# Attention in a hybrid decoder step: the masked chunk first, a running row maximum, value products spread over two rows, two tile banks swapped

## The chip, the cores and the metric

The kernel runs on one core of a Trainium2 chip. The core has TensorE (PE, matmuls; its weight loads are listed as PEld), VectorE (DVE), ScalarE (ACT), GpSimd (POOL) and SyncE (SP), which run side by side and wait for each other through semaphores. Results of matmuls land in eight PSUM banks of 512 fp32 columns. The metric is the time of one execution on the device in microseconds; lower is better.

## The reference, cut to what matters

The program is one inference step with two layers. Each layer runs over a prompt of 2048 tokens (and eight single tokens with their caches). One input projection feeds four head groups: a short convolution, RWKV-7 time mixing, latent attention, and attention into 256 memory tokens; then an output projection and the residual. The part that is changed is the causal latent attention of the prompt, four heads:

```
s = q_lat . ckv + q_rope . krope                     # for every head, query block, key
s = where(kpos <= qpos, s * MLA_SCALE, -1e30)
pr = softmax(s, axis=keys)
o = pr . ckv                                         # then through w_uv, times a SiLU gate
```

The kernel folds w_uk and w_uv into keys and values (`keysT`, 96 rows for each head; `vals`, 64 columns for each head), and it divides by the sum of the exponentials after the products. All data is fp32.

## The kernel before

**Blocks.** A layer goes over the prompt in 8 blocks of 256 tokens. Block number = 2m + e, with m = 0 to 3 and e = 0 or 1, so there are 16 prompt blocks in the program, four for each m. A block is projected (27 tiles of the input projection, `tile`), then comes RWKV in chunks, with the later tiles and the query work put between its steps (`rest`), then the attention, the memory attention and the output projection. Each engine has its own program in the order of its own text; the order is written by hand and is kept by semaphores.

**Attention of a block.** It has 8 rows: `row = 4p + 2j + h`, with p the head pair, j the half of the 256 tokens (128 queries) and h the head of the pair. h = 0 is the even-head row, h = 1 the odd-head row that follows it. A row has m + 1 chunks of up to 512 keys; chunks are counted through, c = 0 to 8(m+1) - 1, and `chunk_of` gives c's row and its key chunk kc. The last key chunk, kc = m, holds the causal diagonal: its width is (2e + j + 1) * 128, and the last 128 columns get a mask (`fmask`). So for e = 0 that chunk is 128 or 256 wide, for e = 1 384 or 512.

For chunk c the work is:
- TensorE, `scores(c)`: one matmul of up to 512 columns (two instructions) into one of five banks. Five are issued ahead; `scores(c + 5)` follows `turn(c)`.
- VectorE, `masked_max(c)`: if it is the masked chunk, add the mask in the bank (L1640); reduce to the maximum of the chunk (L1642); after the row's last chunk reduce over the chunks (L1645) and scale by -MLA_SCALE (L1647), which signals `s_an`, with a drain between these.
- ScalarE, `probs(c)` (L2251): exponential with the row's maximum as bias, into `Sm`. It waits for `s_an` of its row, and so for the scores of all chunks of it.
- TensorE, `turn(c)` (L660): up to four 128x128 transposes of `Sm`.
- ScalarE, `take(c)`: copy of the turned chunk out of PSUM, for an even row to `PTe` (room for whole rows), for an odd row to `PT`, two buffers (L2261). ScalarE's order is probs(0), then for each c probs(c + 1), take(c).
- TensorE, `values(c)`: for a chunk of an odd row the value products of both heads of the pair, up to eight matmuls in two column halves, accumulated in bank 4. On TensorE the order is, for each c: turn(c), scores(c + 5), values(c - 1), so products stand in the odd-head rows alone.

**Banks of the tiles.** Tiles 15 to 24 alternate between banks 6 and 7, `6 + (t - 15) % 2`, so tile 19 is in bank 6, tile 20 in bank 7. In `rest`, just ahead of tile 19 (its eight matmuls begin at s = 34), the latents are turned into bank 7 (s = 28 to 31, read by ScalarE at L2215 and L2216, first `s_krt`) and the value rows are made in bank 6 (s = 32, 33, read at L2222, second `s_krt`). Tile 19 waits for the second, tile 20 for the first. ScalarE does, in this order: L2215, L2216, two DMA issues (L2219), `level(2)` (two copies at L2185, which TensorE's `second_product` of that level waits for), L2222.

On the chip all matmuls stand at L656 (transposes at L660), since a helper records them; the tiles' names tell them apart: `bank<-kv,Q` are scores, `bank<-PT,kv`, `bank<-T,kv`, `bank<-pr,kv` value products, `bank<-cst,Sm` the transposes of probabilities, `bank<-hT,win` the input projection, `bank<-wuv,ckr` the value rows.

Of the kernel before, what the change touches and what calls it, by code (L numbers as in the profile page):

```python
# [15 lines left out]
ACT = mybir.ActivationFunctionType  # L16
AX = mybir.AxisListType.X
MULT, ADD, SUB, POW, MAX, MIN = ALU.mult, ALU.add, ALU.subtract, ALU.pow, ALU.max, ALU.min

P = 128  # L20
# [18 lines left out]
MLA_SCALE = (NOPE + RD) ** -0.5  # L39
# [108 lines left out]
def build_program(nc, a):  # L148
    ctx = ExitStack()
    with ctx:  # L150
# [5 lines left out]
        def sig(name, n, base=0):  # L156

            s = Sig(ctx, nc, name, n, base)
            if base:
# [41 lines left out]
        XX = sb("XX", [P, NH, 2, P])  # L201
# [16 lines left out]
        PP = [ctx.enter_context(nc.psum_tensor(f"bank{i}", [P, 512], F32)) for i in range(8)]  # L218
# [8 lines left out]
        flat4 = lambda t: t[:, :, :, :].rearrange("p a b t -> p (a b t)")  # L227
# [16 lines left out]
        OT = XX[:, :, :, :].rearrange("p h a t -> p h (a t)")  # L244
        ckvN = qd[:, 0, :].rearrange("p (t r) -> p t r", r=R)
        tmax, rmax, rneg = ml[:, 0:32].rearrange("p (r k) -> p r k", k=4), ml[:, 32:40], ml[:, 40:48]
        psum, rsum, rinv = ml[:, 48:80].rearrange("p (r k) -> p r k", k=4), ml[:, 80:88], ml[:, 88:96]
        inv64 = T3[:, :, :].rearrange("p a (b d) -> p (a b) d", d=64)
        whole = lambda t: t[:, :, :].rearrange("p a (b q) -> p a b q", b=2)
        PTe = [[whole(t) for t in (T1, T2, T3, eP)],  # L250
               [pr[:, 2 * i:2 * i + 2, 1:1 + T].rearrange("p a (b q) -> p a b q", b=2) for i in range(3)] + [whole(Ls)]]
# [97 lines left out]
        s_krt = sig("turned_latents_read", 2)  # L349
# [5 lines left out]
        s_an = sig("row_max_ready", 8)  # L355
# [30 lines left out]
        s_av = sig("values_summed", STEPS // 2, base=1)  # L386
# [61 lines left out]

        def chunk_of(c, m):

            row, kc = c // (m + 1), c % (m + 1)
            return row, kc, row // 4, row // 2 % 2, row % 2

        def chunk_width(B, c, m):

# [2 lines left out]

        def copies_of(c, m):

            row, kc, _, _, _ = chunk_of(c, m)
            return row // 2 * (m + 1) + kc

        def score_bank(c):

# [1 line left out]

        def tile_bank(t):

            return t % 4 if t < 15 else 6 + (t - 15) % 2 if t < 25 else 3  # L470

        def steps_before(l, m, e):

# [180 lines left out]
        def _(pe):  # L654
# [28 lines left out]
            def tile(B, t, k0=0, k1=KD):  # L683

                g, i, c, f = TILES[t]
                bank = tile_bank(t)
                if k0 == 0:
                    if i == 0:
                        pe.wait_ge(s_wi[g % 2].h, s_wi[g % 2].at(B.ip, loads_of_slot(g)))
                    if f == 64:  # L690
                        pe.wait_ge(s_kc.h, s_kc.at(B.ip, 1))
                    if 4 <= t < 15:
                        pe.wait_ge(s_pa.h, s_pa.at(B.ip, t - 3))
                    elif t == 15:
                        pe.wait_ge(s_rw.h, s_rw.at(B.it, 1))
                    elif t == 19:
                        pe.wait_ge(s_krt.h, s_krt.at(B.ip, 2))
                    elif t == 20:
                        pe.wait_ge(s_krt.h, s_krt.at(B.ip, 1))
                    elif t == 25:  # L700
                        pe.wait_ge(s_ar[1].h, pairs_done(B))
                    elif t == 26:
                        pe.wait_ge(s_pa.h, s_pa.at(B.ip, t))
                    elif t > 16:
                        pe.wait_ge(s_pa.h, s_pa.at(B.ip, t - 1))
                for k in range(k0, k1):
                    last = mm(PP[bank][0:f, 0:T + B.ns], win[:, g % 2, k, c:c + f], hT[:, k, 0:T + B.ns], k == 0, k == KD - 1)
                if k1 == KD:
                    last.then_inc(s_pj.h, 1)
# [255 lines left out]
            def attention(B, l, m, e):  # L965

                n0, n = steps_before(l, m, e), 8 * (m + 1)

                def scores(c):
                    _, kc, p, j, h = chunk_of(c, m)  # L970
                    w = chunk_width(B, c, m)
                    mm(PP[score_bank(c)][:, 0:w], Q96[:, 2 * p + h, j * P:(j + 1) * P],
                       keysT[:, 2 * p + h, kc * KC:kc * KC + w]).then_inc(s_as.h, 1)

                def turn(c):
                    pe.wait_ge(s_ae.h, n0 + c + 1)
                    if c >= 2:
                        pe.wait_ge(s_ar[chunk_of(c - 2, m)[4]].h, n0 // 2 + copies_of(c - 2, m) + 1)
                    for i in range(chunk_width(B, c, m) // P):
                        last = tr(PP[2 + c % 2][:, i * P:(i + 1) * P], Sm[:, c % 2, i * P:(i + 1) * P], P)  # L980
                    last.then_inc(s_at.h, 1)

                def values(c):
                    _, kc, p, j, h = chunk_of(c, m)
                    if h == 0:
                        return
                    x = copies_of(c, m)
                    pe.wait_ge(s_ar[0].h, n0 // 2 + x + 1)
                    pe.wait_ge(s_ar[1].h, n0 // 2 + x + 1)
                    even, odd = PTe[(2 * p + j) % 2][kc], PT[:, x % 2, :, :]  # L990
                    k = chunk_width(B, c, m) // P
                    o = slice((2 * p + j) * P, (2 * p + j + 1) * P)
                    for i in range(k):
                        first, final = kc == 0 and i == 0, kc == m and i == k - 1
                        v = vals[:, kc * 4 + i, 2 * p * HD:(2 * p + 2) * HD]
                        mm(PP[4][0:HD, o], v[:, 0:HD], even[:, i // 2, i % 2, :], first, final)
                        last = mm(PP[4][HD:P, o], v[:, HD:P], odd[:, i, :], first, final)
                    last.then_inc(s_av.h, 1)
                pe.wait_ge(s_kvd.h, s_kvd.at(B.it, 1))
                pe.wait_ge(s_krt.h, s_krt.at(B.ip, 2))  # L1000
                pe.wait_ge(s_pa.h, s_pa.at(B.ip, NTILES - 2))
                pe.wait_ge(s_yr.h, s_yr.at(B.ip, 4))
                for c in range(5):
                    scores(c)
                for c in range(n):
                    turn(c)
                    if c + 5 < n:
                        scores(c + 5)
                    if c:
                        values(c - 1)  # L1010
                values(n - 1)

            def attention_out(B):

# [269 lines left out]
        def _(v):  # L1284
            def drain():

                v.drain()  # L1287
# [343 lines left out]
            def attention(B, l, m, e):  # L1631

                n0, n = steps_before(l, m, e), 8 * (m + 1)

                def masked_max(c):
                    row, kc, _, _, _ = chunk_of(c, m)
                    w, bank = chunk_width(B, c, m), PP[score_bank(c)]
                    v.wait_ge(s_as.h, n0 + c + 1)
                    if kc == m:
                        v.tensor_tensor(bank[:, w - P:w], bank[:, w - P:w], fmask[:, :], ADD)  # L1640
                        drain()
                    v.tensor_reduce(tmax[:, row, kc:kc + 1], bank[:, 0:w], AX, MAX)  # L1642
                    if kc == m:
                        drain()
                        v.tensor_reduce(rmax[:, row:row + 1], tmax[:, row, 0:m + 1], AX, MAX)  # L1645
                        drain()
                        v.tensor_scalar(rneg[:, row:row + 1], rmax[:, row:row + 1], -MLA_SCALE, None, MULT).then_inc(s_an.h, 1)  # L1647

                for c in range(5):
                    masked_max(c)  # L1650
                for c in range(5, n):
                    masked_max(c)
                v.wait_ge(s_ae.h, n0 + n)
                v.tensor_reduce(rsum, psum[:, :, 0:m + 1], AX, ADD)
                drain()
                v.reciprocal(rinv, rsum)
                v.wait_ge(s_av.h, n0 // 2 + 3 * (m + 1) + s_av.base)
                drain()
                v.tensor_copy(inv64, scalars(rinv, 64)).then_inc(s_on.h, 1)
# [293 lines left out]
        def _(act):  # L1953
# [10 lines left out]
            for l in range(L):  # L1964
# [194 lines left out]
                def block(B, m, e):  # L2159
# [94 lines left out]
                    def take(c):  # L2254
# [1 line left out]
                        x, k = copies_of(c, m), chunk_width(B, c, m) // P  # L2256
                        act.wait_ge(s_at.h, n0 + c + 1 + s_at.base)
                        if h:
                            if x >= 2:
                                act.wait_ge(s_av.h, n0 // 2 + x - 1 + s_av.base)  # L2260
                            act.activation(PT[:, x % 2, 0:k, :], PP[2 + c % 2][:, 0:k * P].rearrange("p (a t) -> p a t", a=k), ACT.Copy)\  # L2261
                                .then_inc(s_ar[1].h, 1)
                            return
                        if 2 * p + j >= 2:
                            act.wait_ge(s_av.h, n0 // 2 + x - 2 * (m + 1) + 1 + s_av.base)
                        o, q = PTe[(2 * p + j) % 2][kc], PP[2 + c % 2][:, 0:k * P].rearrange("p (a t) -> p a t", t=P)
                        if k == 1:
                            last = act.activation(o[:, 0, 0, :], PP[2 + c % 2][:, 0:P], ACT.Copy)
                        elif k == 3:
# [192 lines left out]
```

## Time and profile before

| | |
|---|---|
| time, median of 3 runs | 4077.79 us (4076.91 to 4081.21) |
| profiled execution, its own time | 4085.56 us |
| its span in the profile | 4083.4 us |
| mean granted TensorE clock in it | 0.968 of full speed |
| busy: TensorE, weight loads, VectorE, ScalarE, GpSimd | 3745.4, 2727.1, 1823.1, 1373.2, 145.4 us |
| exponentials of the attention (L2251) | 320 |
| masks (L1640), reductions over a row's chunks (L1645), scalings (L1647) | 128 each |

Each engine's busy time is the sum of its instructions' records. A group of instructions shows after the bar its busy time, the mean of one in ns, and the idle time of the engine just before such instructions, with what ended it. A long idle time matters only where it stands on the engine that sets the pace.

### The profile page before, as it was taken

The page shows a single profiled execution, that of the slowest core. Times are in us where ns is not written, and L with a number is a line of the kernel's source. Part 1 is how long each engine was busy: PE and PEld are TensorE (multiplying, and loading weights), DVE is VectorE, ACT ScalarE, POOL GpSimd, SP SyncE. Part 2 cuts the span into 40 slices and gives each one's busy share as a digit, 9 for nine tenths or more (in the row PEclk, how much of TensorE's full clock was granted, in tenths as well). Part 3 has the DMA queues.
Part 4 walks back from the last instruction along what each step waited for, and adds up shares of the span by engine and source line. Part 5 has one row for each costly group of instructions (what it writes and reads, how often), then busy time and mean ns, then how long its engine had stood idle before and what let it go on. Part 6 is the DMA issues. An engine that isn't in the chain of part 4 may idle for free.

```text
span 4083.4 us, 73861 instructions
## 1 busy us (share of the span) xinstructions
PE 3745.4 (92%) x30760; PEld 2727.1 (67%) x30760; DVE 1823.1 (45%) x3987; ACT 1373.2 (34%) x3579; POOL 145.4 (4%) x278
## 2 busy tenths in 40 slices
PE   4978999999999999999789799999999999999996
PEld 3756767676767667586457477776767686766763
DVE  2544535454544435354325445353535454353542
ACT  1232333334242432434223224233333435234241
POOL 0000000000000000000000000000000000000000
PEclk8988999999999999999889799999999999999998
DMA  6323242423324142231433142524242331523203
GB/s 228 102 88 112 85 157 85 137 86 125 98 93 139 53 158 85 69 121 39 141 125 96 57 143 67 166 65 157 85 137 85 100 122 52 169 65 112 89 27 110
DMA packets 319400, 431.78 MB, mean 106 GB/s; under 512 B 26670, under 2 KB 276460, under 8 KB 318908
## 3 DMA queue, kind: packets, MB, share of 16 engines
q1 hardware_dynamic: 291672, 374.85, 28.7%
q0 software_dynamic: 11648, 41.95, 3.2%
q10 hardware_dynamic: 15748, 10.24, 0.9%
q8 instruction: 245, 4.01, 0.4%
q14 instruction: 87, 0.71, 0.1%
HBM read 405.22 MB, written 32.26 MB: 107 GB/s over the span
## 4 chain that ended last, share of the span: by engine, by line
PE 77%; DVE 8%; DMA 5%; ACT 4%; issue 3%; DVEq 3%; ACTq 1%; POOL 0%; SPq 0%; POOLq 0%
PE bank L656 70%; PE bank L660 7%; DMA wout<-in_w_out 4%; DVEq L1287 3%; DVE T L1391 1%; DVE ml L1642 1%; ACT Sm L2251 1%; DMA win<-in_w_in 0%; ACT PT L2291 0%; ACTq L2219 0%; ACT mix L2148 0%; DVE xin L1710 0%; ACT PT L2103 0%; DVE pr L1399 0%; DVE T L1401 0%
## 5 line engine op out<-in xcount | busy, mean ns | idle before, releaser
L656 PE MATMUL bank<-hT,win 128*128 128x256 f32 (+3 forms) x6912 | 1637.1, 387 | 20.6 <-ACT kv L2222 14.3
L656 PEld LDWEIGHTS bank<-hT,win 128*128 128x128 f32 (+1 forms) x6912 | 1266.8, 189 | 258.7 <-issue 60.9
L656 PE MATMUL bank<-wout,mix 128*128 128x512 f32 x1024 | 459.0, 598 | 35.6 <-DMA wout<-in_w_out 33.2
L656 PEld LDWEIGHTS bank<-wout,mix 128*128 128x128 f32 x1024 | 187.4, 190 | 285.5 <-issue 200.6
L1642 DVE TENSOR_REDUCE ml<-bank 128x1 f32<-128x512 f32 (+3 forms) x320 | 194.9, 610 | 211.6 <-PE bank L656 202.1
L656 PE MATMUL bank<-kv,Q 96*128 96x512 f32 (+3 forms) x640 | 276.8, 531 | 11.2 <-ACT mix L2017 11.2
L660 PE MATMUL bank<-cst,Sm 128*128 128x128 f32 x1344 | 218.8, 284 | 54.6 <-ACT Sm L2251 46.9
L660 PEld LDWEIGHTS bank<-cst,Sm 128*128 128x128 f32 x1344 | 152.5, 141 | 163.1 <-ACT Sm L2251 98.3
L2251 ACT ACTIVATE Sm<-bank,ml 128x512 f32<-128x512 f32 (+3 forms) x320 | 199.7, 624 | 100.2 <-DVE ml L1647 99.0
L1699 DVE TENSOR_TENSOR st<-st 128x1 f32<-128x1 f32 (+1 forms) x34 | 5.4, 159 | 476.0 <-ACT mix L2148 474.5
L2017 ACT ACTIVATE mix<-bank 128x256 f32<-128x256 f32 x128 | 49.1, 384 | 327.8 <-PE bank L656 327.8
L1573 DVE TENSOR_TENSOR XX<-XX,bank 128x512 f32<-128x512 f32 (+1 forms) x160 | 101.5, 634 | 128.3 <-PE bank L656 125.8
L2148 ACT ACTIVATE mix<-bank 128x512 f32<-128x512 f32 (+1 forms) x68 | 39.6, 596 | 340.3 <-PE bank L656 340.3
L656 PE MATMUL bank<-PT,kv 128*64 128x128 f32 x1088 | 154.0, 284 | 0.0
L656 PE MATMUL bank<-PT,XX 64*64 64x64 f32 x2560 | 145.2, 222 | 0.0
L656 PEld LDWEIGHTS bank<-PT,XX 64*64 64x64 f32 x2560 | 119.0, 135 | 23.6 <-issue 21.6
L656 PEld LDWEIGHTS bank<-kv,Q 96*128 96x128 f32 x640 | 100.4, 192 | 39.1 <-issue 35.4
L656 PE MATMUL bank<-XX,PT 64*64 64x64 f32 x2048 | 123.6, 219 | 0.0
L2017 ACT ACTIVATE pr<-bank 128x256 f32<-128x256 f32 x112 | 43.2, 386 | 238.6 <-PE bank L656 238.6
L2002 ACT ACTIVATE hT<-bank,vec 128x128 f32<-128x128 f32 (+1 forms) x272 | 72.4, 378 | 141.5 <-PE bank L660 136.5
L656 PEld LDWEIGHTS bank<-PT,kv 128*64 128x64 f32 x1088 | 117.5, 139 | 0.0
L1332 DVE COPY halo<-pr 128x1 f32<-128x1 f32 (+1 forms) x64 | 10.5, 164 | 234.3 <-ACT pr L2017 233.2
(437 smaller groups left out, 5472.4 us busy)
## 6 DMA issues: line engine op xcount, KB each, us to landing
win<-in_w_in SPq DMA_DIRECT2D x176, 1024.0 KB, 5.3
wout<-in_w_out SPq DMA_DIRECT2D x132, 512.0 KB, 4.3
xin<-out_xres SPq DMA_DIRECT2D x32, 1024.0 KB, 7.7
out_xres<-xin SPq DMA_DIRECT2D x16, 1024.0 KB
win<-in_w_in SPq DMA_DIRECT2D x16, 896.0 KB, 4.9
win<-in_w_in SPq DMA_DIRECT2D x16, 640.0 KB, 4.5
win<-in_w_in SPq DMA_DIRECT2D x16, 512.0 KB, 5.4
bon<-in_cache_mem_k SPq DMA_DIRECT2D x16, 256.0 KB, 3.8
```

The costliest lines, as they stand in the source:

```text
L656: return pe.matmul(out, lhsT, rhs, start=start, stop=stop, skip_group_check=True)
L660: return pe.transpose(out, in_, ident[0:w, 0:w])
L1287: v.drain()
L1332: v.tensor_copy(halo[:, a0:a1], pr[:, a0:a1, n:n + 1].rearrange("p a o -> p (a o)"))
L1391: v.reciprocal(t2, t2)
L1573: v.tensor_tensor(XI[j][:, 0:k, :, :], XI[j][:, 0:k, :, :], d, SUB).then_inc(s_xxr.h, 1)
L1642: v.tensor_reduce(tmax[:, row, kc:kc + 1], bank[:, 0:w], AX, MAX)
L1699: v.tensor_tensor(r, st[0:w, 8 + 2 * j:9 + 2 * j], st[0:w, 9 + 2 * j:10 + 2 * j], ADD)
L2002: last = act.mul(hT[:, dt, cols], PP[bank + dt // 4][:, (dt % 4) * P:(dt % 4) * P + w], V("pre", dt))
L2017: act.activation(o, PP[bank][0:o.shape[0], 0:T], ACT.Copy).then_inc(s_pa.h, 1)
L2148: last = act.activation(junk[0:w, (2 * j + i) * 512:(2 * j + i + 1) * 512], PP[4 + 2 * j + i][0:w, :], ACT.Square, accum_out=st[0:w, 8 + 2 ...
L2251: act.activation(Sm[:, c % 2, 0:w], PP[score_bank(c)][:, 0:w], ACT.Exp, bias=rneg[:, row:row + 1], scale=MLA_SCALE, accum_out=psum[:, row, ...
```

## The change

Four things are changed. (1) `chunk_of` gives the masked key chunk kc = m at the first place of each row, and then kc = 0 to m - 1. (2) `masked_max` keeps a running negative maximum: the first chunk writes `rneg = -scale * top`, each later one `rneg = min(-scale * top, rneg)` with one scalar_tensor_tensor; the reduction over the row's chunks is gone; `s_an` is signalled at the row's last chunk. (3) `values` is called by the number x of the pair of chunks: after every second chunk, when c >= m + 2 and c - m is even, values((c - m)/2 - 1), and what is left after the loop (one pair for m = 0 and 1, two for m = 2 and 3). The odd head's turned probabilities have four buffers instead of two; the new ones lie in `XX`. (4) From tile 19 on the banks 6 and 7 are exchanged: tile 19 goes to bank 7 and waits for the first `s_krt`, tile 20 to bank 6 and waits for the second.

```diff
+        PTo = [PT[:, 0, :, :], PT[:, 1, :, :]] + [flat4(XX)[:, i * 512:(i + 1) * 512].rearrange("p (i t) -> p i t", i=4) for i in range(2)]
...
         def chunk_of(c, m):
-            row, kc = c // (m + 1), c % (m + 1)
-            return row, kc, row // 4, row // 2 % 2, row % 2
+            row, x = c // (m + 1), c % (m + 1)
+            return row, x - 1 if x else m, row // 4, row // 2 % 2, row % 2
...
         def copies_of(c, m):
-            row, kc, _, _, _ = chunk_of(c, m)
-            return row // 2 * (m + 1) + kc
+            return c // (m + 1) // 2 * (m + 1) + c % (m + 1)
...
         def tile_bank(t):
-            return t % 4 if t < 15 else 6 + (t - 15) % 2 if t < 25 else 3
+            return t % 4 if t < 15 else 6 + (t - 15 + (t > 18)) % 2 if t < 25 else 3
...
-                    elif t == 19:
-                        pe.wait_ge(s_krt.h, s_krt.at(B.ip, 2))
-                    elif t == 20:
-                        pe.wait_ge(s_krt.h, s_krt.at(B.ip, 1))
+                    elif t in (19, 20):
+                        pe.wait_ge(s_krt.h, s_krt.at(B.ip, t - 18))
...
-                def values(c):
-                    _, kc, p, j, h = chunk_of(c, m)
-                    if h == 0:
-                        return
-                    x = copies_of(c, m)
+                def values(x):
+                    c = (2 * (x // (m + 1)) + 1) * (m + 1) + x % (m + 1)
+                    _, kc, p, j, _ = chunk_of(c, m)
                     pe.wait_ge(s_ar[0].h, n0 // 2 + x + 1)
                     pe.wait_ge(s_ar[1].h, n0 // 2 + x + 1)
-                    even, odd = PTe[(2 * p + j) % 2][kc], PT[:, x % 2, :, :]
+                    even, odd = PTe[(2 * p + j) % 2][x % (m + 1)], PTo[x % 4]
...
-                        first, final = kc == 0 and i == 0, kc == m and i == k - 1
+                        first, final = x % (m + 1) == 0 and i == 0, x % (m + 1) == m and i == k - 1
...
                     turn(c)
                     if c + 5 < n:
                         scores(c + 5)
-                    if c:
-                        values(c - 1)
-                values(n - 1)
+                    if c >= m + 2 and (c - m) % 2 == 0:
+                        values((c - m) // 2 - 1)
+                for x in range((n - m - 1) // 2, n // 2):
+                    values(x)
...
-                    v.tensor_reduce(tmax[:, row, kc:kc + 1], bank[:, 0:w], AX, MAX)
+                    top, neg = tmax[:, row, kc:kc + 1], rneg[:, row:row + 1]
+                    v.tensor_reduce(top, bank[:, 0:w], AX, MAX)
+                    drain()
                     if kc == m:
-                        drain()
-                        v.tensor_reduce(rmax[:, row:row + 1], tmax[:, row, 0:m + 1], AX, MAX)
-                        drain()
-                        v.tensor_scalar(rneg[:, row:row + 1], rmax[:, row:row + 1], -MLA_SCALE, None, MULT).then_inc(s_an.h, 1)
+                        last = v.tensor_scalar(neg, top, -MLA_SCALE, None, MULT)
+                    else:
+                        last = v.scalar_tensor_tensor(neg, top, -MLA_SCALE, neg, MULT, MIN)
+                    if c % (m + 1) == m:
+                        last.then_inc(s_an.h, 1)
...
                         if h:
-                            if x >= 2:
-                                act.wait_ge(s_av.h, n0 // 2 + x - 1 + s_av.base)
-                            act.activation(PT[:, x % 2, 0:k, :], PP[2 + c % 2][:, 0:k * P].rearrange("p (a t) -> p a t", a=k), ACT.Copy)\
+                            if x >= 4:
+                                act.wait_ge(s_av.h, n0 // 2 + x - 3 + s_av.base)
+                            act.activation(PTo[x % 4][:, 0:k, :], PP[2 + c % 2][:, 0:k * P].rearrange("p (a t) -> p a t", a=k), ACT.Copy)\
...
-                        o, q = PTe[(2 * p + j) % 2][kc], PP[2 + c % 2][:, 0:k * P].rearrange("p (a t) -> p a t", t=P)
+                        o, q = PTe[(2 * p + j) % 2][x % (m + 1)], PP[2 + c % 2][:, 0:k * P].rearrange("p (a t) -> p a t", t=P)
```

## Rows read from the trace of the kernel before

**Rows 1.** The page, busy time, share of the span and instructions of TensorE.
```profile
PE 3745.4 (92%) x30760; PEld 2727.1 (67%) x30760; DVE 1823.1 (45%) x3987; ACT 1373.2 (34%) x3579; POOL 145.4 (4%) x278
```

**Rows 2.** The page, groups: busy, mean ns, idle before, what ended it.
```profile
L656 PE MATMUL bank<-hT,win 128*128 128x256 f32 (+3 forms) x6912 | 1637.1, 387 | 20.6 <-ACT kv L2222 14.3
...
L660 PE MATMUL bank<-cst,Sm 128*128 128x128 f32 x1344 | 218.8, 284 | 54.6 <-ACT Sm L2251 46.9
```

**Rows 3.** Windows, m = 3, e = 0: us; busy PE, PEld, DVE, ACT, POOL; clock.
```profile
1626.50:1686.20 59.70, 52.73 (x388) 32.40 (x388) 24.64 (x59) 36.28 (x97) 0.00 (x0) 1.00 0.07 22
...
3645.00:3706.20 61.20, 54.23 (x388) 33.62 (x388) 24.63 (x59) 36.37 (x97) 0.00 (x0) 0.97 0.06 21
```

**Rows 4.** TensorE's waits in attention, m = 3, 2, 1: us, times, longest.
```profile
PE bank L660 <- ACT Sm L2251: 7.3, 6, 2.0
...
PE bank L660 <- ACT Sm L2251: 2.0, 3, 0.9
...
PE bank L660 <- ACT Sm L2251: 1.0, 2, 0.7
```

**Rows 5.** Timeline at a row edge, m = 3, e = 1: start, us, engine [idle].
```profile
3910.52 0.49 PE L660 MATMUL bank<-cst,Sm 128*128 128x128 f32 x3
...
3910.72 0.30 DVE L1640 TENSOR_TENSOR bank<-bank,fmask 128x128 f32<-128x128 f32 x1 [0.39 <-PE bank L656]
...
3911.10 0.56 DVE L1642 TENSOR_REDUCE ml<-bank 128x1 f32<-128x384 f32 x1
3911.73 0.16 DVE L1645 TENSOR_REDUCE ml<-ml 128x1 f32<-128x4 f32 x1
3911.96 0.15 DVE L1647 TENSOR_SCALAR ml<-ml 128x1 f32<-128x1 f32 x1
...
3912.15 0.69 ACT L2251 ACTIVATE Sm<-bank,ml 128x512 f32<-128x512 f32 x1 [1.48 <-DVE ml L1647]
...
3912.98 0.66 PE L660 MATMUL bank<-cst,Sm 128*128 128x128 f32 x4 [1.10 <-ACT Sm L2251]
```

**Rows 6.** Timeline of TensorE where the scores of that block run out.
```profile
3957.17 0.60 PE L660 MATMUL bank<-cst,Sm 128*128 128x128 f32 x4
3957.61 1.02 PE L656 MATMUL bank<-kv,Q 96*128 96x512 f32 x2
3958.47 0.60 PE L660 MATMUL bank<-cst,Sm 128*128 128x128 f32 x4
3961.07 0.66 PE L660 MATMUL bank<-cst,Sm 128*128 128x128 f32 x4 [1.99 <-ACT Sm L2251]
...
3962.22 0.93 PE L660 MATMUL bank<-cst,Sm 128*128 128x128 f32 x4 [0.50 <-ACT Sm L2251]
```

**Rows 7.** Timeline of TensorE, transposes of two chunks of an odd-head row.
```profile
3916.75 0.66 PE L660 MATMUL bank<-cst,Sm 128*128 128x128 f32 x4
...
3919.22 0.55 PE L660 MATMUL bank<-cst,Sm 128*128 128x128 f32 x3
```

**Rows 8.** Timeline of VectorE, m = 0, e = 0: reductions of two rows.
```profile
219.76 0.29 DVE L1642 TENSOR_REDUCE ml<-bank 128x1 f32<-128x128 f32 x1
...
220.79 0.29 DVE L1642 TENSOR_REDUCE ml<-bank 128x1 f32<-128x128 f32 x1
```

**Rows 9.** Timeline of ScalarE and TensorE around tile 19.
```profile
3856.73 0.22 ACT L2216 ACTIVATE kro<-bank 128x64 f32<-128x64 f32 x1
...
3857.42 1.13 PE L656 MATMUL bank<-wuv,ckr 128*128 128x256 f32 x4
...
3857.98 0.66 ACT L2185 ACTIVATE PT<-bank 128x256 f32<-128x256 f32 x2 [1.03 <-PE bank L656]
...
3858.59 0.60 ACT L2222 ACTIVATE kv<-bank 128x512 f32<-128x512 f32 x1
...
3859.33 0.67 PE L656 MATMUL bank<-hT,win 128*128 128x256 f32 x2 [0.78 <-ACT kv L2222]
3859.93 0.33 PE L656 MATMUL bank<-PT,XX 64*64 64x64 f32 x4
```

## The prediction

> **What bounds the kernel now.** I read the page's busy shares first: TensorE is busy 3745 us, 92% of the span [rows 1], so only its idle time, or work taken from it, can pay. The change takes no matmul away. The second view is the page's groups with what ended the idle time before them. Two groups belong to the change: the transposes of the probabilities waited 46.9 us for the exponential of ScalarE, and the input projections 14.3 us for ScalarE's copy of the value rows [rows 2]. Third, the windows of single attentions: with m = 3, TensorE is busy 52.7 of 59.7 us, VectorE 24.6, ScalarE 36.3 [rows 3]. No engine but TensorE is near full, so what is missing is lost to latency. Fourth, the waits of single attentions: 7.3 us in six waits for m = 3, 2.0 us in three for m = 2, 1.0 us in two for m = 1, each for the odd block (e = 1) of its m [rows 4]. They are few and long, so the timeline tells where each one sits.
>
> **One row edge, m = 3.** The transposes of the row's last chunk but one end a pass of scores at 3910.52; the score bank just filled is the masked, last chunk of the next row. Its maximum needs the mask at 3910.72, the reduction at 3911.10, the reduction over chunks at 3911.73 and the scaling at 3911.96; the exponential starts at 3912.15, and TensorE goes on at 3912.98: a chain of 2.46 us [rows 5]. Meanwhile TensorE issued three transposes and one score. How long these take is read where nothing waits: four transposes 0.44 us (3957.17 to 3957.61), so three 0.33, and a score of 512 keys 0.86 (3957.61 to 3958.47) [rows 6]. That leaves 1.27 us idle. The row's 1.10 is less because a matmul's record runs on after its issue. After an odd-head row there is no such wait, since value products stand there: a chunk with them takes 2.47 us (3916.75 to 3919.22) [rows 7], one without 1.30, so the products of one pair are 1.17 us.
>
> **Row maximum.** Removed from the chain after a row's last score: mask with its gap (3910.72 to 3911.10, 0.38 us) and the second reduction with its gap (3911.73 to 3911.96, 0.23) [rows 5], 0.61 in all. The running minimum takes the place of the scaling; no row shows a scalar_tensor_tensor of this size, its bounds are nothing and a full 0.23 us more, and I take no difference, since it is a 128x1 operation as both of its neighbours are (0.16 and 0.15). The mask is now added at the row's first chunk, hidden behind the scores of the others. The last chunk is 512 wide: for e = 1 that adds 0 to 0.13, for e = 0 up to 0.40 (0.69 against 0.29 for 128 columns [rows 8]). The first exponential is that of the narrow chunk, 0.1 to 0.3 shorter. So for m = 3, e = 1: 2.46 - 0.61 + 0.13 - 0.11 = 1.87.
> Every unmasked chunk gains one small operation and a drain, 192 times in all (320 - 128). At 0.23 us that is 44 us of VectorE. It is hidden: a reduction of 0.69, and 0.23 behind it, make 0.92 us a chunk, against 1.30 of TensorE. If that cover were gone, it would eat the whole gain.
>
> **Products spread.** They stand after every second chunk, from chunk m+2 on. For m = 3 that is each odd chunk, so every row edge has cover 0.44 + 0.86 + 1.17 = 2.47 against 1.87. The edges at chunks 12 and 20 vanish, 1.27 each. At chunk 4 no product is there yet: 1.87 - 1.30 = 0.57 stay, 0.70 gained. At chunk 28 scores are used up; from 3958.47 to 3961.07 the chain is 2.60, cover 0.44, idle 2.16 [rows 6]. After: 1.99 - (0.44 + 1.17) = 0.38, gained 1.78. Then the price: three pairs are left behind the last transposes where there were two, and the last transposes run at ScalarE's pace, copy 0.60 [rows 9] and exponential 0.69 [rows 5]. Without products beside them chunks 29 and 31 wait about 0.96 and 0.66 (an estimate from these durations), where 0.7 is lost now (3961.07 + 0.44 to 3962.22): 0.9 lost. The opening wait (five scores, then the first row's chain) is worth 0.1, since VectorE now has mask and reduction in front of three more reductions. Sum for e = 1: 2.54 + 0.70 + 1.78 - 0.90 + 0.10 = 4.2. For e = 0 the same with 0.5 at chunk 4 and 0.4 for the whole tail: 3.5. Four such attentions: 15.4 us.
> m = 2: the scores run out at chunk 18, and the longest wait, 0.9 [rows 4], before chunk 21, is ScalarE's pace, not a maximum. The pair that stood at chunk 18 moves to chunk 20 and fills it: 1.1 for e = 1, 0.7 for e = 0; four attentions 3.6. m = 1: likewise the pair of chunk 12 goes to 13 and fills 0.7 [rows 4], a little more for e = 0; four: 3.2. m = 0: the place of the products stays. For e = 0 VectorE is the pace, 1.03 us a row (219.76 to 220.79) [rows 8], and loses 0.23 in each of eight rows: at most 1.84, I take 1.5 as ScalarE and TensorE come near; for e = 1 ScalarE is almost as slow, 0.7. Four: 4.4. Attention in all 26.6 us; ends 14 (only the two middle edges of m = 3 and a third of the rest) and 55 (all 46.9 and some 8 of matmul ends that the records hide). Buffers cost nothing: with four odd-head buffers the products that free one are always at least four chunks back.
>
> **Banks.** The value rows are issued at 3857.42 into bank 6 (four matmuls, 0.87), and tile 19 wants bank 6 too. It starts at 3859.33, after level(2) at 3857.98 and the copy at 3858.59; without the wait it could start at 3858.29, 1.04 earlier [rows 9]. Now it goes to bank 7, whose read ended at 3856.95. What is late next: the second product at 3859.93 would come at 3858.89 and needs level(2)'s first copy, half of 0.66 from 3857.98, so 3858.31 [rows 9]; it holds. Tile 20 needs the copy of value rows, two levels later. Sixteen blocks: 16.0, ends 12.5 (the visible 0.78 alone) and 16.6; if the wait goes to level(2) wholly, nothing.
> No DMA is moved and no queue passed; nothing new waits on SP's or POOL's.
>
> **Sum.** 26.6 + 16.0 = 42.6 us. The profiled execution took 4085.6 us (span 4083.4 and 2.2 around it), so 4043.0; the median of the runs is 7.8 lower, 4077.8, so 4035.
>
> **Rivals.**
> Attention keeps most of its waits: ScalarE's copies and exponentials are in one order, and the rows open late because an exponential waits ahead of a copy. For: ScalarE's pace of 1.30 equals TensorE's without products. Against: over two chunks TensorE has 3.77, ScalarE 2.6. Gain 10 + 16: 4052. Chance 0.17.
> Bank swap gives nothing, the wait goes to level(2): 4051. Against it the times above. Chance 0.06.
> The clock helps: two of the four m = 3 attentions show 1.00 and 0.97 for the same work, 59.7 and 61.2 us [rows 3], with the long waits of the tail in both. Fewer waits could spare such falls to 1.2 GHz there and at the close of m = 0, some 1.5 to 3 us each, 8 in all: 4027 or lower. Against: the new tail still waits. The Trainium skill, TensorE: Matmul & The Clock Gate, Why this matters for your kernels, says likewise that idle gaps between bursts of matmuls bring the slow clock back. Chance 0.12.
> The other side: VectorE becomes the pace. Each of 192 unmasked chunks then costs 0.23 on the path, 44 us, the edges' gain goes with it and the banks give 16: 4106. It decides if an unmasked chunk takes VectorE more than 1.30 us, against 0.92 from the rows. Chance 0.03. The Trainium skill, VectorE: DVE Perf Modes, Rules for kernel authors, speaks for this side: it says to keep the number of chained operations on VectorE small, and the change has 64 more (192 added, 128 taken), which at 0.23 each would be 15 us lost; the 24.6 busy of 59.7 us [rows 3] speaks against the rule here.
> The change does nothing measurable (waits go elsewhere after attention): 4074. Chance 0.02.
>
> **How the numbers follow.** Forecast 4035, chance 0.60 (4028 to 4047). The range takes in both partial rivals and half of the clock's: 4020 to 4057. A change of under 0.2% (8 us) can hardly be told from none here; faster 0.95, same 0.02, slower 0.03.
>
> **What the profile would show.** Transposes' wait for the exponential near 20 us, not 46.9; no 14.3 us wait for the copy of value rows; waits at chunks 12 and 20 gone for m = 3, at 4 halved, two short ones in the tail; VectorE's total about 10 us more, with 64 more instructions. Wrong would be: new waits for level(2)'s copies, or VectorE not idle between unmasked chunks.

## The result and the profile after

| | before | after |
|---|---|---|
| time, median of 4 runs | 4079.5 us (4076.9 to 4081.3) | 4024.1 us (4020.3 to 4025.7) |
| profiled execution, its own time | 4085.6 us | 4023.5 us |
| span, mean granted clock | 4083.4 us, 0.968 | 4021.4 us, 0.971 |

The ratio is 0.9863 (95% interval 0.9846 to 0.988): 55.4 us faster, where 42.6 were forecast (4035). The time lies inside the range given (4020 to 4057), but below the forecast's own band (4028 to 4047), where the clock's rival had put it (4027 or lower). The two profiled executions are 62.0 us apart in span, and the stretches below add up to that. Run once more in a later group, the changed kernel had a median of 4020.9 us, 61.8 under the kernel before in that group; one of its four executions there took 8600.9 us, in the slow state, and is left out of the ratio.

The page of the changed kernel, busy time and the two groups of [rows 1, 2]:

```profile
PE 3727.1 (93%) x30760; PEld 2727.1 (68%) x30760; DVE 1832.4 (46%) x4051; ACT 1369.7 (34%) x3579; POOL 145.3 (4%) x278
...
L656 PE MATMUL bank<-hT,win 128*128 128x256 f32 (+3 forms) x6912 | 1636.9, 387 | 4.5 <-ACT hT L2002 4.5
...
L660 PE MATMUL bank<-cst,Sm 128*128 128x128 f32 x1344 | 215.4, 282 | 27.0 <-ACT Sm L2251 19.1
```

The transposes wait 19.1 us for the exponential, not 46.9; the wait for the copy of the value rows, 14.3 us, is gone. VectorE has 64 instructions and 9.3 us more. These two waits alone are 42.1 us less. TensorE's busy time fell by 18.3 us though its instructions are the same 30760. That is the first sign that the clock has a share.

Windows of the changed kernel, m = 3: two attentions with e = 0, then one with e = 1 (us; busy PE, PEld, DVE, ACT, POOL; clock), as in [rows 3]:

```profile
1606.97:1662.43 55.46, 52.40 (x388) 32.67 (x388) 27.06 (x75) 35.28 (x97) 0.00 (x0) 1.00 0.07 23
3596.11:3651.59 55.48, 52.42 (x389) 32.69 (x389) 27.07 (x75) 35.30 (x97) 0.00 (x0) 1.00 0.07 24
1856.36:1917.91 61.55, 58.97 (x436) 36.49 (x436) 29.48 (x75) 39.58 (x99) 0.00 (x0) 1.00 0.03 13
```

They were 59.7 and 61.2 us for e = 0; they are now equal, at full clock. TensorE's waits of the third, where [rows 4] had 7.3 us in six:

```profile
PE bank L660 <- ACT Sm L2251: 2.5, 4, 1.3
```

The four left are the opening (before the first transposes) 1.25, and 0.42, 0.36 and 0.50: chunk 4, chunk 28 and the one behind it. At chunks 12 and 20 there is none. Chunk 12's edge in that attention, VectorE, ScalarE and TensorE in order of time, against [rows 5]:

```profile
1879.79 0.60 PE L660 MATMUL bank<-cst,Sm 128*128 128x128 f32 x4
...
1879.99 0.69 DVE L1640 TENSOR_REDUCE ml<-bank 128x1 f32<-128x512 f32 x1 [1.55 <-PE bank L656]
...
1880.76 0.16 DVE L1645 SCALAR_TENSOR_TENSOR ml<-ml 128x1 f32<-128x1 f32 x1
1880.95 0.69 ACT L2251 ACTIVATE Sm<-bank,ml 128x512 f32<-128x512 f32 x1 [1.23 <-DVE ml L1645]
...
1880.97 0.32 PE L656 MATMUL bank<-eP,kv 128*64 128x128 f32 x1
...
1881.99 0.66 PE L660 MATMUL bank<-cst,Sm 128*128 128x128 f32 x4
```

The transposes that end the score pass start at 1879.79 and the exponential starts at 1880.95; with 0.83 to TensorE, as in [rows 5], the chain is 1.99 us, where 2.46 was and 1.87 was predicted. TensorE has products meanwhile (`bank<-eP,kv` at 1880.97, and others) and comes to the transposes at 1881.99, 0.21 after they could start.

Around tile 19, the stretch of [rows 9]:

```profile
3802.87 0.22 ACT L2216 ACTIVATE kro<-bank 128x64 f32<-128x64 f32 x1
...
3803.56 1.13 PE L656 MATMUL bank<-wuv,ckr 128*128 128x256 f32 x4
...
3804.12 0.66 ACT L2185 ACTIVATE PT<-bank 128x256 f32<-128x256 f32 x2 [1.03 <-PE bank L656]
...
3804.53 0.59 PE L656 MATMUL bank<-hT,win 128*128 128x256 f32 x2
3804.73 0.60 ACT L2222 ACTIVATE kv<-bank 128x512 f32<-128x512 f32 x1
...
3805.05 0.33 PE L656 MATMUL bank<-PT,XX 64*64 64x64 f32 x4
```

From the value rows' matmuls to tile 19 it was 1.91 us (3857.42 to 3859.33). It is now 0.97. ScalarE's copy at 3804.73 now runs behind the tile's matmuls. The second product comes 1.49 after the value rows, not 2.51: it moved 1.02 forward with the tile.

**Where 62.0 us went.** The 16 attention windows (first score to first score of the memory attention) sum to 590.0 us before and 552.3 after: 37.7, of it 23.4 for m = 3, 5.6 for m = 2, 3.2 for m = 1, 5.5 for m = 0. The stretch from the value rows to the next attention is 1.02 shorter in most of the 16 blocks, which would be 16.3; all 16 together are 19.1 shorter, since one block gained 3.4. The remaining 5.2 lie in other stretches.

### The profile page after: what moved, and what is told of

It is laid out like the page before. It is cut to its first block, busy times and chain, and to the rows that moved or that the text cites. A ratio compares the mean times of both kernels' runs of the same rounds, so it can differ in the third digit from the quotient of the medians.

```text
span 4021.4 us, 73957 instructions
## 1 busy us (share of the span) xinstructions
PE 3727.1 (93%) x30760; PEld 2727.1 (68%) x30760; DVE 1832.4 (46%) x4051; ACT 1369.7 (34%) x3579; POOL 145.3 (4%) x278
## 4 chain that ended last, share of the span: by engine, by line
PE 79%; DVE 7%; DMA 5%; ACT 3%; DVEq 3%; issue 2%; ACTq 0%; POOL 0%; SPq 0%; POOLq 0%
PE bank L656 71%; PE bank L660 7%; DMA wout<-in_w_out 5%; DVEq L1284 3%; DVE T L1388 1%; DVE ml L1640 1%; ACT PT L2291 0%; ACT Sm L2251 0%; DVE xin L1710 0%; ACT mix L2148 0%; ACT PT L2103 0%; DVE pr L1396 0%; DVE T L1391 0%; DVE T L1400 0%; DVE T L1398 0%
## 5 line engine op out<-in xcount | busy, mean ns | idle before, releaser
L660 PE MATMUL bank<-cst,Sm 128*128 128x128 f32 x1344 | 215.4, 282 | 27.0 <-ACT Sm L2251 19.1
L656 PEld LDWEIGHTS bank<-PT,XX 64*64 64x64 f32 x2560 | 118.4, 135 | 24.0 <-issue 15.9
L656 PEld LDWEIGHTS bank<-kv,Q 96*128 96x128 f32 x640 | 100.7, 193 | 37.4 <-issue 33.4
L1533 DVE TENSOR_TENSOR OO<-OO,cst 128x256 f32<-128x256 f32 x160 | 67.8, 424 | 97.4 <-PE bank L656 94.8
L656 PEld LDWEIGHTS bank<-XX,PT 64*64 64x64 f32 x2048 | 102.3, 135 | 0.0
```

The source lines that it names most:

```text
L656: return pe.matmul(out, lhsT, rhs, start=start, stop=stop, skip_group_check=True)
L660: return pe.transpose(out, in_, ident[0:w, 0:w])
L1533: v.tensor_tensor(Om[j], An[j], mlev[:, lev + 1:lev + 2, :].broadcast_to([P, NH, 64]), MULT).then_inc(s_om.h, 1)
```

## The experiments

Differences in us are between medians of one group of runs on one chip; a ratio's 95% interval is some 7 us to either side. The kernel before had 4081.9 in the first group, 4082.6 in the second, 4081.6 in the third. The changed kernel run again in the second had 4020.9 (0.9847, 0.9828 to 0.9867). Attention windows are from the profiled executions.

**Banks alone (4), on the kernel before.**

```diff
-            return ... 6 + (t - 15) % 2 if t < 25 else 3
+            return ... 6 + (t - 15 + (t > 18)) % 2 if t < 25 else 3
...
+                    elif t in (19, 20):
+                        pe.wait_ge(s_krt.h, s_krt.at(B.ip, t - 18))
```

> The kernel before with only the two tile banks exchanged. Theory (the wait of tile 19 is really gone, and what else the change gained is the attention's): TensorE's wait for the copy of the value rows falls from 14.3 us to 0, no wait for level(2)'s copies comes, 1.0 us in each of 16 blocks: 16 us faster, 4062. Rival (the wait turns up again later in the inverse's levels): under 5 us faster. Second rival (the wait is gone and the clock also gains by it): 18 to 21.

Measured 4061.4, ratio 0.9947 (0.9931 to 0.9964): 20.5 us. Attention windows 591.4, so nothing there; TensorE's waits in attention (us in total, times, longest) are those of before:

```profile
PE bank L660 <- ACT Sm L2249: 47.0, 56, 2.0
```

**All but the banks (1 to 3).** The changed kernel with edit (4) undone.

> The full change without the exchange of banks: both attention parts. Theory: 38 us of attention and about 3 of clock after m = 0: 38 to 42 faster, 4039; less than the sum of the two alone (44), since they cover the same waits at m = 3's edges. With the swap alone it adds up to the full change (55). Rival (the bank exchange brings more beside the others than alone): under 35.

Measured 4040.2, ratio 0.9901 (0.9885 to 0.9918): 41.7 us. Attention windows 552.5, as with the swap, and the wait for the value rows is back, in 16 blocks:

```profile
PE bank L656 <- ACT kv L2224: 14.8, 16, 1.9
```

20.5 and 41.7 make 62.2; the whole change has 55.4 and, in the second group, 61.8. Within the intervals the parts add, and the attention windows do not depend on the banks.

**Row maximum and masked chunk first (1, 2), products where they stood.**

```diff
-                    if c >= m + 2 and (c - m) % 2 == 0:
-                        values((c - m) // 2 - 1)
+                    if c:
+                        values(c - 1)
+                values(n - 1)
```

The cut shows the order of the products only, against the changed kernel; two odd-head buffers and the old banks come with it.

> Only the masked chunk first and the running negative maximum; products in the odd-head rows and banks as before. Theory (row maximum and products cover the same waits, so that either alone has more than its share): the three edges of m = 3 still wait 0.6 each, the last one 1.5; m = 0 gains as in the full change (2.5 and 0.5 a block). 18 us faster, 4061. Rival (the running maximum is the part that brings the attention's 38 us): 30 or more. Rival (VectorE's small operations cost): under 5.

Measured 4059.8, 0.9947 (0.993 to 0.9963): 22.1 us, where 18 were expected; windows 573.7, 16.3 less than before.

**Products spread (3) alone,** with their four buffers, on the old row order and maximum. The cut shows their order against the kernel before.

```diff
-                    if c:
-                        values(c - 1)
+                    if c >= m + 2 and (c - m) % 2 == 0:
+                        values((c - m) // 2 - 1)
```

> Only the products spread over two rows, with four buffers; masked chunk last, maximum over the row's chunks, banks as before. Theory: a row edge of m = 3 has cover 2.47 against a chain of 2.46, so the middle edges vanish by this alone; nothing at m = 0; m = 1 and 2 as in the full change. 26 us faster, 4053. Rival (without the shorter chain the edges keep a wait): 12 to 18.

Measured 4065.0, 0.9958 (0.9941 to 0.9974): 16.9 us, not the 26 expected; the rival's 12 to 18 held. Windows 575.9, 14.1 less. TensorE's waits in the attention with m = 3, e = 1, row maximum alone and then products alone:

```profile
PE bank L660 <- ACT Sm L2254: 4.7, 6, 1.4
```

```profile
PE bank L660 <- ACT Sm L2250: 5.0, 7, 1.4
```

With the row maximum alone six waits stay (0.74 at chunk 12, 1.39 at 28); with products alone the chain is still 2.46 and the cover too short at chunk 4 (1.10), at 12 (0.33) and at 28 (1.19). Only together do edges 12 and 20 close in all four. 16.3 and 14.1 are 30.4, both at once 37.7. The 7.3 us over the sum belong to neither alone, and most of them are not at m = 3 (us saved in four attention windows each):

| | row maximum alone | products alone | both |
|---|---|---|---|
| m = 3 | 10.0 | 10.7 | 23.4 |
| m = 2 | 0.9 | 3.0 | 5.6 |
| m = 1 | 0.5 | 0.5 | 3.2 |
| m = 0 | 4.8 | -0.1 | 5.5 |

Up to 1.5 of the 7.3 can be the clock: the windows hold 15.9 us of half clock in the kernel before, 5.6 with the row maximum alone, 13.2 with the products alone and none with both.

**Row order without the running minimum.** The changed kernel, but the reduction over chunks and the scaling at the row's end again.

```diff
-                    drain()
-                    if kc == m:
-                        last = v.tensor_scalar(neg, top, -MLA_SCALE, None, MULT)
-                    else:
-                        last = v.scalar_tensor_tensor(neg, top, -MLA_SCALE, neg, MULT, MIN)
                     if c % (m + 1) == m:
-                        last.then_inc(s_an.h, 1)
+                        drain()
+                        v.tensor_reduce(rmax[:, row:row + 1], tmax[:, row, 0:m + 1], AX, MAX)
+                        drain()
+                        v.tensor_scalar(neg, rmax[:, row:row + 1], -MLA_SCALE, None, MULT).then_inc(s_an.h, 1)
```

> The changed kernel with the masked chunk first, but the maximum over the row's chunks taken at the row's end as before (a second reduction and a scaling in place of the running minimum). Theory (each 0.23 us in the chain behind a row's last score counts where a wait is left, so in m = 0, e = 0 and in the openings and the fourth chunk of m = 3): m = 0, e = 0 loses 1.8 a block, m = 3 about 0.6, the others 0.2 to 0.4: 9 us slower than the changed kernel. Rival (the running minimum brings nothing, the mask's place alone does): within 3.

Measured 4034.1 (4029.2 to 4035.5), 0.9883 (0.9867 to 0.99): 13.2 us slower than the changed kernel beside it, where 9 were expected. Windows 562.5, 10.1 longer. For m = 0, e = 0 it is 12.06 against 9.78 us, since VectorE is the pace there and does one operation more in each of eight rows; 1.0 us at half clock at its end adds up to 0.5. For m = 3 it is 1.4 us (e = 0) and 0.5 to 0.7 (e = 1). In the attention with m = 3, e = 1:

```profile
PE bank L660 <- ACT Sm L2249: 3.0, 4, 1.3
```

**More small operations on VectorE.** The running minimum is done three times on each unmasked chunk but a row's last, the same result; 192 operations and drains more, about 44 us of VectorE.

```diff
+                        if c % (m + 1) < m:
+                            for _ in range(2):
+                                v.scalar_tensor_tensor(neg, top, -MLA_SCALE, neg, MULT, MIN)
+                                drain()
                         last = v.scalar_tensor_tensor(neg, top, -MLA_SCALE, neg, MULT, MIN)
```

> The changed kernel with the running minimum done three times instead of once on every unmasked chunk that is not its row's last: 192 more small operations with their drains, 44 us of VectorE, none in the chain behind a row's last score; the result stays the same. Theory (VectorE's small operations are hidden behind TensorE): within 5 us of the changed kernel, most of it in the openings of m = 2 and 3, where five scores stand alone. Rival (they are on the path): 30 to 44 us slower than the changed kernel.

Measured 4035.9 (4029.9 to 4037.7), 0.9883 (0.9866 to 0.9899): 15.0 us slower than the changed kernel, against at most 5 expected. The miss has two parts. The timeline of the opening of an attention (m = 3, e = 1), whose scores begin at 1861.71:

```profile
1864.47 0.40 DVE L1647 SCALAR_TENSOR_TENSOR ml<-ml 128x1 f32<-128x1 f32 x2
...
1867.28 0.58 ACT L2255 ACTIVATE Sm<-bank,ml 128x384 f32<-128x384 f32 x1 [5.12 <-DVE ml L1649]
...
1868.00 0.55 PE L660 MATMUL bank<-cst,Sm 128*128 128x128 f32 x3 [2.19 <-ACT Sm L2255]
```

and the changed kernel's, which begins at 1856.36:

```profile
1861.00 0.58 ACT L2251 ACTIVATE Sm<-bank,ml 128x384 f32<-128x384 f32 x1 [4.18 <-DVE ml L1645]
...
1861.72 0.55 PE L660 MATMUL bank<-cst,Sm 128*128 128x128 f32 x3 [1.25 <-ACT Sm L2251]
```

In the opening nothing hides VectorE: five scores are issued, and the first row's chain is 0.93 us longer (5.57 against 4.64 to the exponential). After it the extra operations cost nothing: from chunk 2 to the last, 30 chunks, the two kernels keep the same distance. The second part is the clock, below. Windows of the two attentions with m = 3, e = 0 of this kernel:

```profile
1609.46:1667.52 58.06, 54.09 (x388) 33.62 (x389) 31.92 (x107) 35.30 (x97) 0.00 (x0) 0.97 0.07 23
3605.17:3661.54 56.37, 52.40 (x388) 32.63 (x388) 31.63 (x107) 35.25 (x97) 0.00 (x0) 1.00 0.07 25
```

The second is 0.9 longer than the changed kernel's (55.48), the opening alone; the first 1.7 more than that, with one fall of the clock. The attentions lose 10.2 us in all, 8.8 of it for m = 3 and the rest for m = 2; those with m = 0 and 1, which have no such chunk, lose nothing. The other 4.7 lie outside, two falls of the clock among them (one in the changed kernel).

**Two odd-head buffers instead of four.**

```diff
-                            if x >= 4:
-                                act.wait_ge(s_av.h, n0 // 2 + x - 3 + s_av.base)
-                            act.activation(PTo[x % 4] ...
+                            if x >= 2:
+                                act.wait_ge(s_av.h, n0 // 2 + x - 1 + s_av.base)
+                            act.activation(PTo[x % 2] ...
```

> The changed kernel with two buffers for the odd head's turned probabilities, as before, in place of four. Theory (products lag behind the copies, so two buffers are too few for m = 3 alone): the copy of the odd-head row's fourth chunk must wait for products that TensorE issues only after that chunk's transposes, some 1 to 2 us in each of four pairs of rows, hidden in part: m = 3 loses 3 to 6 us a block, m = 0 and 1 nothing, 10 to 22 us slower than the changed kernel (4021 to 4024). Rival (the four buffers bring nothing): within 3.

Measured 4024.4 (4021.5 to 4027.6), 0.9862 (0.9845 to 0.9878): within 4 us of the changed kernel of either group, so the rival (within 3) is nearer than 10 to 22. Attention windows are 5.0 us longer, all for m = 3 (1.5 and 1.8 for e = 0, 0.9 twice for e = 1); the rest of that execution was shorter by 4.5 to 7 than in the changed kernel's two profiled executions, which nothing here explains. ScalarE does wait for products to free a buffer (m = 3, e = 0: wait, times, longest), a wait that the changed kernel lacks there:

```profile
ACT PT L2261 <- PE bank L656: 2.6, 4, 1.4
```

but of these 2.6 us only 1.5 reach the attention's length; ScalarE had slack for the rest.

**One step on: the wait for tile 24's copy moved behind two scores.** The changed kernel waited there 0.68 us in each block before its first score, though the first two scores do not use that copy's buffers.

```diff
-                pe.wait_ge(s_pa.h, s_pa.at(B.ip, NTILES - 2))
                 pe.wait_ge(s_yr.h, s_yr.at(B.ip, 4))
                 for c in range(5):
+                    if c == 2:
+                        pe.wait_ge(s_pa.h, s_pa.at(B.ip, NTILES - 2))
                     scores(c)
```

> The changed kernel with TensorE's wait for the copy of tile 24 moved from ahead of the attention's first score to ahead of the third one, the first that writes into a bank of the tiles. Theory: the 0.68 us wait at the start of every attention (10.9 us in all) and the tail of the last matmul before it are filled by two scores: 0.85 in each of 16 blocks, 12 to 14 us faster than the changed kernel. Rival (the row's maximum is as late as before, so the wait moves to the first transposes): 0 to 4.

Measured 4007.2 (4004.7 to 4010.2), 0.9817 (0.9801 to 0.9834): 13.7 us faster than the changed kernel, 75.5 than the kernel before: the best version. The changed kernel, then this one, at the same block's first scores:

```profile
3845.51 0.38 ACT L2017 ACTIVATE mix<-bank 128x256 f32<-128x256 f32 x1 [3.07 <-PE bank L656]
...
3846.15 4.10 PE L656 MATMUL bank<-kv,Q 96*128 96x384 f32 x10 [0.68 <-ACT mix L2017]
```

```profile
3829.77 3.71 PE L656 MATMUL bank<-kv,Q 96*128 96x384 f32 x9
3829.97 0.38 ACT L2018 ACTIVATE mix<-bank 128x256 f32<-128x256 f32 x1 [3.07 <-PE bank L656]
```

Scores stood 0.64 behind the start of the copy, now 0.20 ahead of it: 0.84 a block, 13.4 in 16.

## Why the prediction was right or wrong, by its own steps

**Banks, 16.0: right.** 1.04 a block was worked out, 1.02 is what most blocks' stretches show. Level(2)'s copy did not take the wait over, with one exception below. In one block the kernel before waited longer, and 3.4 us were gained there instead of 1.02:

```profile
1583.26 1.09 PE L656 MATMUL bank<-hT,win 128*128 128x256 f32 x2 [2.45 <-ACT kv L2222]
```

The reason is the second DMA issue, which stands on ScalarE ahead of level(2): least, median and most ns, in the kernel before and in the changed one:

```profile
L2219 ACTq DMA_DIRECT2D out_krope<-kro x16: 487/488/2217, 174.6 to 3857.4; - x16
```

```profile
L2219 ACTq DMA_DIRECT2D out_krope<-kro x16: 485/488/1827, 174.0 to 3803.5; - x16
```

In that block it took 2.22 us (from 1579.65) instead of 0.49, and the copies behind it came 1.7 late. In the changed kernel it took 1.83 in the same block, and TensorE waited 0.8 for level(2)'s copy in front of the second products there, the only such wait of the program. The 2.45 us wait also had a fall of the clock right behind it (3.4 us at 1.2 GHz from 1583.4), which the changed kernel lacks. With the banks alone the 16 stretches are 17.9 us shorter, of the 18.7 between that profiled execution and the one before.

**One row edge: right but for 0.12.** The scalar_tensor_tensor costs what the scaling did: its rows on VectorE, against the scaling of a row's first chunk (durations in ns, least, median, most):

```profile
L1645 DVE SCALAR_TENSOR_TENSOR ml<-ml x192: 158/159/163, 697.8 to 3899.8; 128x1 f32<-128x1 f32 x192
L1643 DVE TENSOR_SCALAR ml<-ml x128: 152/153/155, 218.5 to 3894.0; 128x1 f32<-128x1 f32 x128
```

The 0.12 is the exponential of chunk 12, 512 wide in this row: I had taken off 0.11 for a narrow one.

**m = 3, e = 1, 4.2 predicted: 5.3 without the clock.** By the chunks in front of which the time was gained, measured (and predicted): opening 0.40 (0.10), chunk 4 0.47 (0.70), chunk 12 1.56 (1.27), chunk 20 1.10 (1.27), chunk 28 1.77 (1.78), tail about 0 (-0.90), and 1.2 more by the clock. For e = 0 it is 4.24 at full clock in both kernels, 3.5 predicted: opening and chunk 4 1.1 (0.6), chunks 12 and 20 2.3 (2.5), chunk 28 and the tail 0.9 (0.4).

**The term that was mis-sized most is the tail of e = 1.** I let it run at ScalarE's pace of 0.60 + 0.69 = 1.29 a chunk and charged 0.9. ScalarE and TensorE there in the changed kernel:

```profile
1911.41 0.69 ACT L2251 ACTIVATE Sm<-bank,ml 128x512 f32<-128x512 f32 x1
...
1912.07 0.60 ACT L2261 ACTIVATE PT<-bank 128x512 f32<-128x512 f32 x1
1912.55 0.70 ACT L2251 ACTIVATE Sm<-bank,ml 128x512 f32<-128x512 f32 x1
```

```profile
1909.10 0.60 PE L660 MATMUL bank<-cst,Sm 128*128 128x128 f32 x4
...
1911.09 0.66 PE L660 MATMUL bank<-cst,Sm 128*128 128x128 f32 x4 [0.36 <-ACT Sm L2251]
1912.24 0.66 PE L660 MATMUL bank<-cst,Sm 128*128 128x128 f32 x4 [0.50 <-ACT Sm L2251]
...
1913.85 1.36 PE L660 MATMUL bank<-cst,Sm 128*128 128x128 f32 x8
```

Exponentials start 1.14 apart (1911.41, 1912.55): the second starts before the record of the copy ahead of it ends. And the wait behind chunk 28 was there before the change too ([rows 6]: 0.50, and here 0.50). From chunk 28 to the end of the attention it is 6.86 us with the old product order (row maximum alone) and 6.83 with the new: for e = 1 spreading costs the tail nothing. For e = 0 the tail did get longer, at full clock 6.00 us before, 6.42 with the row maximum alone, 6.61 in the changed kernel; two thirds of it come with the row maximum and the masked chunk first, so that wide chunks end the row. The Trainium skill, ScalarE: Activation LUTs, What ACT_TABLE_LOAD costs, says that back-to-back activations overlap by about 93 ns; this trace is near that for the copy and the exponential behind it (1912.07 + 0.60 - 1912.55 = 0.12).

**The other sizes.** m = 1 gave 3.2, as predicted, but the reason was only half right: the spread products were to bring it by filling a wait that is ScalarE's pace, and alone they bring 0.5. They need the new row order and maximum beside them; which chunk needs which was not followed, so that the number fits is in part luck. m = 2 gave 5.6 against 3.6, and 3.0 of it with the products alone: each of the four attentions saved somewhat more than its one wait. m = 0 5.5 against 4.4, of which up to 2.8 can be clock (5.6 us of those windows of the kernel before were at half clock). So the attention's own gain is 30.6 to 33.4 where 26.6 was predicted: mechanism right for m = 3 and 0, size low by 4 to 7, of which the tail (0.9 in each attention with e = 1, and with chunk 28 0.5 in each with e = 0) and m = 2 are the largest known parts.

**VectorE not the pace: right, with one exception.** VectorE's total is 9.3 us more, where about 10 was forecast, and the tripled operations cost nothing over 30 chunks of an attention. The exception is the opening, where the prediction saw only a 0.1 gain. The rule that the prediction set against the change (the Trainium skill, VectorE: DVE Perf Modes, Rules for kernel authors: keep the number of operations small) is not borne out where another engine sets the pace, and is borne out in the opening, with 0.93 us each.

**The clock: a rival at 0.12 that came on top of the forecast.** An m = 3, e = 1 attention of the kernel before, windows up to and in one fall of the clock:

```profile
1881.48:1941.50 60.02, 53.26 (x356) 31.15 (x356) 26.07 (x56) 34.87 (x89) 0.00 (x0) 1.00 0.03 12
1941.80:1945.20 3.40, 3.15 (x22) 2.42 (x22) 0.08 (x1) 3.24 (x9) 0.00 (x0) 0.50 0.00 0
```

0.50 is 1.2 GHz. The fall follows a wait of 1.99 us at chunk 28. Away from the layers' starts and ends the kernel before has six such falls, 27.3 us at 1.2 GHz; the changed one has 3.4 us. Work at half speed loses half its time, so this is at most 11.9 us. Three of the falls stood inside m = 3 attentions; the changed kernel has none there. The kernel with more work on VectorE brings the pattern back: its openings wait 2.19 us, and in three of its four m = 3 attentions the clock was 0.50 for 3.4 us behind that,

```profile
1869.00:1872.00 3.00, 3.00 (x8) 1.53 (x7) 1.17 (x4) 1.98 (x6) 0.00 (x0) 0.50 0.00 0
```

at 1.7 us a fall (58.06 against 56.37 above). The same attention with and without a fall differs by 1.5 us in the kernel before (61.2 and 59.7) and by 1.3 and 1.6 in the two with one part of the change. On what the prediction named (the Trainium skill, TensorE: Matmul & The Clock Gate, Why this matters for your kernels), the traces agree in direction, though the waits here are shorter than the gaps that its row warns of. The fourth wait of 2.19 us had no fall behind it, nor had one of 1.94 in the kernel before, so a wait makes a fall likely, not certain.

**The sum.** The 37.7 us of the attention windows are 30.6 to 33.4 of waits and 4.3 to 7.1 of clock (4.3 of it at m = 3). The banks bring 16.3 and the clock outside attention up to 4.0. The late DMA issue of one block adds 0.8 (its wait was 1.67 over the usual 0.78 before, and 0.84 is still lost in the changed kernel). That is up to 58.8 of the 62.0 between the profiled executions; at least 3.2 are not traced. The forecast was low since the clock was left out of the sum, with the tail and m = 2 as the next parts.

**Open:** why the DMA issue of one block took 1.8 to 2.2 us; how the parts share the gain of m = 1 and m = 2; whether the falls at the close of m = 0 come from its waits. No run held every wait and changed the clock alone; the clock's share is read from windows and is an upper bound, and only the price of a fall is shown, by the same attention in one kernel.

## What to carry to other kernels

Two remedies for one latency (a shorter chain, more cover) must be costed together: each alone left part of the edges open, and 7.3 of 37.7 us came only with both. When a part's number comes out right, run the part alone: for m = 1 it gave 0.5 of the 3.2 put down to it. Extra small operations were free where another engine set the pace, but look at the openings, where there is nothing to hide them. A wait of 2 us on TensorE cost its own length here and, in most cases, 1.3 to 1.7 us of half clock behind it. And read the pace of a chain of operations from start to start, not from summed durations.

## What the runs showed of the hardware that was not expected

- After waits of 1.94 to 2.19 us in m = 3 attentions TensorE's clock fell to 1.2 GHz for 3.4 us: in three of four of the kernel before, in all four with the banks alone, in three of four with more work on VectorE. One fall cost 1.3 to 1.7 us. The changed kernel's waits there, at most 1.3 us, were followed by none. There is no sharp edge between: with products alone one fall followed a wait of 1.57 us and the same wait in the other attention had none; with the row maximum alone one followed two waits of 1.18 and 0.72 in a row, and the same pair in the other attention had none.
- ScalarE's copy and exponential of 512 columns, 0.60 and 0.69 by their records, follow each other at 1.14 us a pair, though a read of the accumulator (0.21) stands between them.
- A DMA issue on ScalarE's queue, 0.49 us in most blocks, took 2.22 us in one block of the kernel before and 1.83 in the same block of the changed one, and everything behind it on ScalarE came that much later.
